# Rows for all partitions: products with a broadcast operand replaced by transfers inside the chip

## The chip, the cores and the metric

The kernel runs on one core of a Trainium2 chip. The metric is the device time of one execution in microseconds (us). All data are 32-bit floats.

## The reference

Two blocks run one after the other on x of [256 tokens, 1024]. What the change touches is this part of the first block (two layers) and of the second (one layer):

```python
# first block, per layer: forgetting attention (4 heads), beside differential and stick-breaking attention
logf = log_sigmoid(bf + b_forget[layer])
cum_logf = cumsum(logf, axis=1).transpose(0, 2, 1)          # [head, position]
logits = q @ k.T * scale + cum_logf[..., :, None] - cum_logf[..., None, :]
p = softmax(where(causal, logits, -inf))

# second block: state space heads (16 heads, chunks of 128), beside an attention with an index and a relative bias
acum = cumsum(dt * a, axis=1)
seg = acum[:, :, None] - acum[:, None, :]
lmat = exp(where(causal, seg, -inf))
wmat = cb[..., None] * lmat * dt[:, None]
y = einsum('bijgh,bjghp->bighp', wmat, x)                   # and the state carried from chunk to chunk

# attention of the second block: logits = q @ k.T * scale + rel_bias[bucket(t - s)], on the 64 best keys by an index
# then: x = x + g_f * moe(h), 32 experts of 1024 x 2048 and 1024 x 1024 each, four per token
```

Both parts need a row vector (a cumulative sum over the keys or the tokens of one head) beside a column vector on every one of the 128 partitions.

## The kernel before

Each engine has one program written out in order (`@block.tensor`, `@block.sync`, `@block.gpsimd`, `@block.scalar`, `@block.vector`); they meet at semaphores. Tokens are handled as two blocks of 128, features as chunks of 128 partitions. TensorE writes its results to seven PSUM banks used in turn: `take(name)` gives the next bank and waits until what it held seven takes ago is freed, `full(mm, name)` tells the others that it is ready, `ch.free(ins, name)` gives it back, `product(engine, name)` makes an engine wait for it.

Weights come in 2 MB groups through a ring of four slots. SP issues them in one written order (L1332 to L1336), each as soon as the group that held its slot was used (`slot_last`). The expert loads follow on the same queue; each waits for products of the mixer part or of earlier experts. Nine slots hold weights of experts.

*First block, per layer.* TensorE makes the projections, then the cumulative sums of the forget gate: `cumq` (the sum as a column, L771 to L773) and, for each of four heads, a [128, 256] bank with the sum as a row on all partitions: the operand `logf[:, b, h:h+1].broadcast_to([P, P])` against a triangular matrix (L779, L781, two heads to a bank, `cumk0` and `cumk1`). DVE makes `sf` from them (L1928), adds the mask, adds the stick-breaking sums `after0` to `after3` to `zs` (L1937) and the strict mask (the event `c_exponent`, for which ScalarE waits), and then adds the q k products `f0` to `f3` to `sf` (L1942). Maxima, exponents on ScalarE, division, and `turn_head(l, "f", h)` on TensorE (L548) follow. The value products of the differential heads are `head_value(l, "a", h)` (L554).

*Second block, state space stage.* `acumT` has the cumulative sums with heads on partitions (copied by DVE at L2025). A loop over p = 0 to 8 has, on TensorE, two products that copy the rows of heads 2p and 2p + 1 to all partitions (`A0` to `A15`, L969), then a projection of other work (`project_aside(p)`: q, kv, index keys, z), then the values of heads 2p - 2 and 2p - 1 (`ssm_values`). On DVE the same loop has `decay_in` for two heads (three operations on A each), then `decay_out` for the two heads before. ScalarE takes the exponents between the two, and copies what the asides made. Before this loop ScalarE copies `x_tok` out of four banks.

*The relative bias.* A [8, 512] table is written by POOL to DRAM 128 times (`bias_scratch`, source `biasrev` on eight partitions of `nine`), and SP loads it shifted into `bm` behind the weight group x2 (L1340 to L1348). DVE adds it near 581 us.

Of the kernel before, what the change touches and what calls it, by code (L numbers as in the profile page):

```python
# [86 lines left out]
def mixer_moe_kernel(nc, a, out):  # L87
# [23 lines left out]
    def sb(name, shape, dt=F32, where=ctx):  # L111
        return where.enter_context(nc.sbuf_tensor(name, shape, dt))
# [113 lines left out]
    mod_part = sb("mod_part", [P, 3, 512], where=first)  # L226
    pick_row = sb("pick_row", [P, 64], where=first)
    x_stats = sb("x_stats", [P, NB, 2, 6], where=first)
    x_mean = sb("x_mean", [P, NB, 2], where=first)
# [21 lines left out]
    bm = sb("bm", [P, 8, W3], where=second)  # L251
    cbs = early[:, NB * D:NB * D + 2 * W3].rearrange("p (g n) -> p g n", g=2)
    idx = sb("idx", [P, 4, W3], where=second)
    probT2 = idx[:, 0:2, :]
# [222 lines left out]
    def _(pe):  # L477
# [238 lines left out]
        for l in range(DEPTH):  # L716
# [57 lines left out]
            full(mm, f"{L}cumq")  # L774
            for h in range(HB):
                if h % 2 == 0:
                    bank = take(f"{L}cumk{h // 2}")
                c = h % 2 * T
                pe.matmul(bank[:, c:c + T], logf[:, 0, h:h + 1].broadcast_to([P, P]), up_ones[:, :],  # L779
                          start=True, stop=False)  # L780
                mm = pe.matmul(bank[:, c + P:c + T], logf[:, 1, h:h + 1].broadcast_to([P, P]), up,  # L781
                               start=False, stop=True)
                if h % 2:
                    full(mm, f"{L}cumk{h // 2}")
            pe.wait_ge(ev("log_fail"), l + 1)
# [175 lines left out]
        for p in range(SH // 2 + 1):  # L961
            if p < SH // 2:
                for h in (2 * p, 2 * p + 1):
                    if h == 0:
                        read_out(pe, "acumT")
                    bank = take(f"A{h}")
                    q = slice(32 * (h % 2), 32 * (h % 2) + 32)
                    at = 32 * (h % 2) + h
                    mm = pe.matmul(bank[:, 0:T], ident[q, at:at + 1].broadcast_to([32, P]), acumT[q, :],  # L969
                                   start=True, stop=True)  # L970
                    full(mm, f"A{h}")
                project_aside(p)
            if p == 1:
                read_out(pe, "xt11")
            if p >= 1:
                for h in (2 * p - 2, 2 * p - 1):
                    ssm_values(h)
# [349 lines left out]
    def _(sp):  # L1327
# [4 lines left out]
        for g, (name, src) in enumerate(groups):  # L1332
# [4 lines left out]
            if g == 1:  # L1337
                sp.dma_start(const_tiles[False][:, P:], packs[False][1][:, P:]).then_inc(ev("const_in"), 16)
                sp.dma_start(const_tiles[True][:, :], packs[True][1][:, :]).then_inc(ev("const_in"), 16)
            if name == "x2":  # L1340
                sp.wait_ge(ev("bias_out"), 16)
                sp.wait_ge(ev("h_ready"), 4 * DEPTH)
                for qb in range(NB):
# [108 lines left out]
    def _(act):  # L1452
# [82 lines left out]
        for l in range(DEPTH):  # L1535
# [36 lines left out]
            for b in range(NB):  # L1572
                read(f"{L}va{b}", va[:, b, :])
            read(f"{L}cv0", vbc[:, 0, 256:512], cols=slice(0, 256))
            act.wait_ge(ev("c_exponent"), l + 1)
# [49 lines left out]
        for i in range(2):  # L1625
            read(f"g{i}", ga[:, 2 * i:2 * i + 2, :])
        act.wait_ge(ev("xs"), 1)
        for b in range(NB):
# [141 lines left out]
    def _(dve):  # L1770
# [109 lines left out]
        for l in range(DEPTH):  # L1880
# [42 lines left out]
            ch.free(dve.tensor_copy(cumq[:, :], product(dve, f"{L}cumq")[:, 0:NB * HB]), f"{L}cumq")  # L1923
            for h in range(HB):
                name = f"{L}cumk{h // 2}"
                cum = product(dve, name)[:, h % 2 * T:(h % 2 + 1) * T]
                ts(sf[:, h, 0:P], cum[:, 0:P], -1.0, cumq[:, h:h + 1], ALU.mult, ALU.add)
                ins = dve.tensor_scalar(sf[:, h, P:W3], cum, -1.0, cumq[:, HB + h:HB + h + 1], ALU.mult, ALU.add)  # L1928
                if h % 2:
                    ch.free(ins, name)  # L1930
                else:
                    ch.after(ins)
            tt(sf[:, :, :], sf[:, :, :], over(K["row_mask"][:, :], HB), ALU.add)

            for h in range(HC):
                name = f"{L}after{h}"
                ch.free(dve.tensor_tensor(zs[:, h, :], product(dve, name)[:, 0:W3], zs[:, h, :], ALU.add), name)  # L1937
            tt(zs[:, :, :], zs[:, :, :], over(K["strict_add"][:, :], 4), ALU.add, ev("c_exponent"))

            for h in range(HB):  # L1940
# [103 lines left out]
        def decay_in(h):  # L2044

            A, d = product(dve, f"A{h}"), decay[:, h % 4, :]
            if h >= 4:
                dve.wait_ge(*values_done[("ssm", h - 4)])
            col = K["col_mask"][:, 0:P]
            stt(d[:, 0:P], A[:, 0:P], neg_acum[:, 0, h:h + 1], col, ALU.add, ALU.add)  # L2050
            ts(d[:, P:T], A[:, P:T], neg_acum[:, 2, h:h + 1], None, ALU.add)
            ch.free(dve.scalar_tensor_tensor(d[:, T:W3], A[:, P:T], neg_acum[:, 1, h:h + 1], col, ALU.add, ALU.add),
                    f"A{h}")
            ch.after(dve.tensor_copy(sink[:, :], d[:, 0:1]), ev("decay_exponent"))

# [264 lines left out]
```

## Time and profile before

| | |
|---|---|
| median of 3 runs | 1632.63 us (1631.58 to 1634.78) |
| the profiled execution | 1630.76 us, span 1628.8 us |
| mean granted TensorE clock | 0.995 of full speed |
| bytes read from DRAM | 511.21 MB, 316 GB/s over the span |
| first block | 0 to 376 us |
| second block up to the experts | 376 to 704 us |
| experts | 704 to 1623 us |

The span is the time from the first to the last instruction in the profile. PE is TensorE, PEld its weight loads, DVE VectorE, ACT ScalarE, POOL GpSimd; SPq, ACTq and POOLq are queues that issue transfers. A matmul of 32-bit data has several records ("x2" and "x4" count records). "Idle before" is the time that an engine stood still before an instruction, and the name behind the arrow is what it waited for.

### The profile page before, as it was taken

To read this page: it belongs to the slowest core of one execution; us is meant where nothing else is said; L and a number is where in the kernel's file an instruction comes from. 1 tells how busy PE (TensorE), PEld (TensorE's weight loads), DVE (VectorE), ACT (ScalarE), POOL (GpSimd) and SP (SyncE) were. 2 spreads that over 40 slices of the span, in tenths; PEclk is the share of its full clock that TensorE was granted. 3 is DMA by queue.
4 is the path that set the end of the run, shared out by engine and by line. 5 is a ranking of instruction groups with operands and counts; after the bars stand their busy time and mean duration, and the time that the engine had idled before them with its cause. 6 is when DMAs were issued, how large, how long until landed. Compare 5 with 4: busy or idle time off the path is not lost.

```text
span 1628.8 us, 18474 instructions
## 1 busy us (share of the span) xinstructions
PE 1544.0 (95%) x7521; PEld 873.4 (54%) x7521; DVE 451.1 (28%) x974; ACT 278.1 (17%) x552; POOL 21.4 (1%) x42
## 2 busy tenths in 40 slices
PE   7999999999999999999999999999999998999997
PEld 6768777786877878843333333333333333333232
DVE  2453643513346471131211111121112112111111
ACT  1244104324232531030000000000000000000000
POOL 4000000000000000000000000000000000000000
PEclk9999999999999999999999999999999999999999
DMA  9763994327333423689999999999999999999996
GB/s 260 194 203 104 339 333 153 107 103 256 128 118 104 144 93 136 280 336 421 428 429 425 428 428 426 430 426 429 427 429 427 426 429 426 430 425 428 426 427 292
DMA packets 84073, 515.19 MB, mean 316 GB/s; under 512 B 5444, under 2 KB 8804, under 8 KB 59440
## 3 DMA queue, kind: packets, MB, share of 16 engines
q1 hardware_dynamic: 81744, 511.35, 77.3%
q0 software_dynamic: 2240, 3.02, 1.9%
q8 instruction: 42, 0.69, 0.2%
q14 instruction: 15, 0.12, 0.0%
q10 hardware_dynamic: 32, 0.01, 0.0%
HBM read 511.21 MB, written 3.15 MB: 316 GB/s over the span
## 4 chain that ended last, share of the span: by engine, by line
PE 77%; DMA 15%; DVE 4%; ACT 2%; issue 1%; SPq 0%; ACTq 0%; another core or an unknown queue 0%; DVEq 0%
PE psum L514 25%; PE psum L1190 20%; PE psum L1287 11%; DMA ring<-in_w_gu 9%; DMA w_down<-in_w_gu 4%; PE psum L1168 4%; PE psum L523 4%; PE psum L1177 2%; PE psum L1135 2%; PE psum L554 1%; DMA ring<-in_w_ada 1%; DMA ring<-in_w_in 1%; PE psum L579 1%; DVE hidden L2266 1%; PE psum L1275 1%
## 5 line engine op out<-in xcount | busy, mean ns | idle before, releaser
L514 PE MATMUL psum<-spare,ring 128*128 128x256 f32 x1504 | 335.3, 382 | 2.8 <-ACT spare L1502 2.7
L514 PEld LDWEIGHTS psum<-spare,ring 128*128 128x128 f32 x1504 | 284.9, 191 | 51.6 <-issue 12.2
L1190 PE MATMUL psum<-ring,hg 128*64 128x512 f32 x1040 | 233.1, 596 | 6.5 <-DMA ring<-in_w_gu 6.5
L1190 PEld LDWEIGHTS psum<-ring,hg 128*64 128x64 f32 x1040 | 71.0, 137 | 155.2 <-issue 140.0
L1190 PE MATMUL psum<-w_down,hg 128*64 128x512 f32 x656 | 146.3, 596 | 4.7 <-DMA w_down<-in_w_gu 4.6
L2257 DVE TENSOR_SCALAR gu<-psum 128x512 f32<-128x512 f32 x32 | 22.1, 691 | 325.3 <-PE psum L1190 325.3
L2269 DVE TENSOR_TENSOR o_slot<-psum,gain_rows 128x512 f32<-128x512 f32 x32 | 22.1, 691 | 320.3 <-PE psum L1287 320.3
L1190 PEld LDWEIGHTS psum<-w_down,hg 128*64 128x64 f32 x656 | 44.9, 137 | 97.6 <-issue 88.6
L1287 PE MATMUL psum<-ring,hiddenT 128*64 128x512 f32 x352 | 78.0, 595 | 9.5 <-ACT hiddenT L1737 7.2
L1287 PE MATMUL psum<-w_down,hiddenT 128*64 128x512 f32 x352 | 78.0, 595 | 9.5 <-ACT hiddenT L1737 7.2
L1731 ACT ACTIVATE putT<-psum 128x256 f32<-128x256 f32 x32 | 12.3, 383 | 381.7 <-PE psum L1197 381.6
L1733 ACT ACTIVATE hidden<-gu 128x512 f32<-128x512 f32 x32 | 20.2, 630 | 297.9 <-DVE gu L2257 297.9
L1168 PEld LDWEIGHTS psum<-pick,h_tok 128*128 128x128 f32 x512 | 60.0, 196 | 11.7 <-issue 11.4
L1177 PE MATMUL psum<-o_slot,putT 64*128 64x512 f32 x256 | 63.6, 615 | 0.8 <-DVE o_slot L2269 0.8
L1168 PE MATMUL psum<-pick,h_tok 128*128 128x128 f32 x512 | 63.0, 283 | 0.2 <-DVE passes L2221 0.2
L523 PE MATMUL psum<-ring,spare 128*128 128x260 f32 (+2 forms) x192 | 56.9, 453 | 0.5 <-DMA ring<-in_w_in 0.5
L514 PE MATMUL psum<-yT,ring 128*128 128x256 f32 x256 | 55.6, 379 | 0.0
L1287 PEld LDWEIGHTS psum<-ring,hiddenT 128*64 128x64 f32 x352 | 26.2, 137 | 54.2 <-issue 54.2
L1287 PEld LDWEIGHTS psum<-w_down,hiddenT 128*64 128x64 f32 x352 | 26.2, 137 | 54.2 <-issue 54.2
L514 PEld LDWEIGHTS psum<-yT,ring 128*128 128x128 f32 x256 | 48.6, 190 | 6.6
L523 PEld LDWEIGHTS psum<-ring,spare 128*128 128x128 f32 x192 | 35.9, 190 | 18.7 <-issue 14.3
L1177 PEld LDWEIGHTS psum<-o_slot,putT 64*128 64x128 f32 x256 | 22.0, 186 | 41.9 <-issue 40.2
(421 smaller groups left out, 1457.7 us busy)
## 6 DMA issues: line engine op xcount, KB each, us to landing
ring<-in_w_gu SPq DMA_DIRECT2D x65, 2048.0 KB, 28.3
w_down<-in_w_gu SPq DMA_DIRECT2D x41, 2048.0 KB, 28.4
ring<-in_w_in SPq DMA_DIRECT2D x24, 2048.0 KB, 9.5
w_down<-in_w_dn SPq DMA_DIRECT2D x22, 2048.0 KB, 28.7
ring<-in_w_dn SPq DMA_DIRECT2D x22, 2048.0 KB, 31.6
ring<-in_w_ada SPq DMA_DIRECT2D x12, 2048.0 KB, 8.9
spare<-in_w_gu SPq DMA_DIRECT2D x11, 2048.0 KB, 28.2
nine<-in_w_gu SPq DMA_DIRECT2D x11, 2048.0 KB, 29.7
```

The costliest lines, as they stand in the source:

```text
L514: mm = pe.matmul(bank[0:m, c * T:(c + 1) * T], w[:, k, c0 + c * P:c0 + c * P + m], src[:, k, :], start=(i == 0), stop=(i == k_n - 1))
L523: mm = pe.matmul(bank[:, 0:n], src[:, k, blk * P:(blk + 1) * P], w[:, k, c0:c0 + n], start=(k == 0), stop=(k == k_n - 1))
L554: pe.matmul(bank[rows, c * T:(c + 1) * T], v[:, 0, cols], wT[:, 0:T], start=True, stop=False)
L579: mm = pe.matmul(bank[:, 0:T], ones_d, wide[:, c, :], start=(c == 0), stop=(c == KC - 1))
L1135: pe.matmul(psum[:, loop_bank(4 + part), :], bias_row[r, side, :, :].rearrange("p h s -> p (h s)"), b_gu[r, :], start=True, stop=False, sk ...
L1168: mm = pe.matmul(psum[:, loop_bank(first_bank + part), j * P:j * P + width * CAP], h_tok[:, b, c * P:(c + 1) * P], pick[:, b, 0:width, :], ...
L1177: mm = pe.matmul(psum[:, loop_bank(2 * b + half), :], putT[r, side, b * P:(b + 1) * P], o_slot[r, :], start=False, stop=False, skip_group_ ...
L1190: mm = pe.matmul(psum[half * CAP:(half + 1) * CAP, loop_bank(4 + part), :], hg[:, k, side, :], w[:, c0:c0 + 512], start=False, stop=(k == ...
L1287: mm = pe.matmul(psum[half * CAP:(half + 1) * CAP, loop_bank(7), :], hiddenT[:, c, j * CAP:(j + 1) * CAP], tile[:, c0:c0 + 512], start=(k ...
L1733: act.activation(hidden[:, 0, :], gu[:, 0, :], ACT.Sigmoid, scale=1.702).then_inc(ev("g_sig"), 1)
L2257: dve.tensor_scalar(gu[:, 0, :], psum[:, loop_bank(4), :], 7.0, None, ALU.min).then_inc(ev("g_in"), 1)
L2269: dve.tensor_tensor(o_slot[:, :], psum[:, loop_bank(7), :], gain_rows[:, :], ALU.mult).then_inc(ev("o_slot"), 1)
```

## The change

In a layer of the first block one bank `cumk` takes the place of two: two products make the sums of all four heads as four rows. ScalarE copies the rows to SBUF (`forget_rows`, partitions 0 to 3 of `lam_in`), then issues four transfers, each of which reads one row 128 times and writes it to all partitions (`forget_all`, in the buffer `qk`). DVE handles `zs` first, then waits for the four transfers and makes `sf` from `forget_all`. In the second block the sixteen `A` products go; ScalarE issues sixteen such transfers from rows 0 to 15 of `acumT`, twelve into `bm` and four into `k2`, ahead of its copies of `x_tok`. DVE waits for four heads at a time. The small copy to `sink` in `decay_in` goes, and the load of the relative bias moves from behind group x2 to behind group kvup, after the twelfth `decay_exponent`, since `bm` is in use until then.

```diff
--- before.py
+++ after.py
@@ -225,6 +225,8 @@
     cumq = sb("cumq", [P, NB * HB], where=first)
     mod_part = sb("mod_part", [P, 3, 512], where=first)
     pick_row = sb("pick_row", [P, 64], where=first)
+    forget_rows = lam_in[:, :, :].rearrange("p a b -> p (a b)")[0:HB, 0:T]
+    forget_all = qk[:, 0:HB, :]
     x_stats = sb("x_stats", [P, NB, 2, 6], where=first)
     x_mean = sb("x_mean", [P, NB, 2], where=first)
     x_rstd = sb("x_rstd", [P, NB], where=first)
@@ -250,6 +252,8 @@
     x_tok = early[:, 0:NB * D].rearrange("p (b d) -> p b d", b=NB)
     bm = sb("bm", [P, 8, W3], where=second)
     cbs = early[:, NB * D:NB * D + 2 * W3].rearrange("p (g n) -> p g n", g=2)
+    A_late = k2[:, :, :]
+    A_first = bm[:, :, :].rearrange("p h n -> p (h n)").rearrange("p (h t) -> p h t", t=T)
     idx = sb("idx", [P, 4, W3], where=second)
     probT2 = idx[:, 0:2, :]
     decay = idx
@@ -772,16 +776,10 @@
             pe.matmul(bank[:, HB:2 * HB], ones, logf[:, 0, :], start=True, stop=False)
             mm = pe.matmul(bank[:, HB:2 * HB], up, logf[:, 1, :], start=False, stop=True)
             full(mm, f"{L}cumq")
-            for h in range(HB):
-                if h % 2 == 0:
-                    bank = take(f"{L}cumk{h // 2}")
-                c = h % 2 * T
-                pe.matmul(bank[:, c:c + T], logf[:, 0, h:h + 1].broadcast_to([P, P]), up_ones[:, :],
-                          start=True, stop=False)
-                mm = pe.matmul(bank[:, c + P:c + T], logf[:, 1, h:h + 1].broadcast_to([P, P]), up,
-                               start=False, stop=True)
-                if h % 2:
-                    full(mm, f"{L}cumk{h // 2}")
+            bank = take(f"{L}cumk")
+            pe.matmul(bank[0:HB, 0:T], logf[:, 0, :], up_ones[:, :], start=True, stop=False)
+            mm = pe.matmul(bank[0:HB, P:T], logf[:, 1, :], up, start=False, stop=True)
+            full(mm, f"{L}cumk")
             pe.wait_ge(ev("log_fail"), l + 1)
             for h in range(HC):
                 bank = take(f"{L}after{h}")
@@ -960,15 +958,6 @@
 
         for p in range(SH // 2 + 1):
             if p < SH // 2:
-                for h in (2 * p, 2 * p + 1):
-                    if h == 0:
-                        read_out(pe, "acumT")
-                    bank = take(f"A{h}")
-                    q = slice(32 * (h % 2), 32 * (h % 2) + 32)
-                    at = 32 * (h % 2) + h
-                    mm = pe.matmul(bank[:, 0:T], ident[q, at:at + 1].broadcast_to([32, P]), acumT[q, :],
-                                   start=True, stop=True)
-                    full(mm, f"A{h}")
                 project_aside(p)
             if p == 1:
                 read_out(pe, "xt11")
@@ -1337,9 +1326,9 @@
             if g == 1:
                 sp.dma_start(const_tiles[False][:, P:], packs[False][1][:, P:]).then_inc(ev("const_in"), 16)
                 sp.dma_start(const_tiles[True][:, :], packs[True][1][:, :]).then_inc(ev("const_in"), 16)
-            if name == "x2":
+            if name == "kvup":
                 sp.wait_ge(ev("bias_out"), 16)
-                sp.wait_ge(ev("h_ready"), 4 * DEPTH)
+                sp.wait_ge(ev("decay_exponent"), 12)
                 for qb in range(NB):
                     width = (qb + 1) * P
                     src = bass.AP(tensor=bias_dram[:, :, :].tensor, offset=T - 1 - qb * P,
@@ -1571,6 +1560,10 @@
             f(small[:, 8:16], small[:, 8:16], ACT.Ln, ev("forget_ln"), bias=1.0)
             for b in range(NB):
                 read(f"{L}va{b}", va[:, b, :])
+            read(f"{L}cumk", forget_rows, cols=slice(0, T), rows=slice(0, HB))
+            for h in range(HB):
+                act.dma_start(forget_all[:, h, :], forget_rows[h:h + 1, :].rearrange("o (x t) -> o x t", x=1).broadcast_to([1, P, T]))\
+                    .then_inc(ev("forget_rows"), 16)
             read(f"{L}cv0", vbc[:, 0, 256:512], cols=slice(0, 256))
             act.wait_ge(ev("c_exponent"), l + 1)
             f(zs[:, :, :], zs[:, :, :], ACT.Exp, ev("wc"))
@@ -1624,6 +1617,10 @@
         f(dtx[:, 3, :], dtx[:, 2, :], ACT.Ln, ev("dt_ln"))
         for i in range(2):
             read(f"g{i}", ga[:, 2 * i:2 * i + 2, :])
+        read_out(act, "acumT")
+        for h in range(SH):
+            A = A_first[:, h, :] if h < 12 else A_late[:, h - 12, :]
+            act.dma_start(A, acumT[h:h + 1, :].rearrange("o (x t) -> o x t", x=1).broadcast_to([1, P, T])).then_inc(ev(f"decay_rows{h // 4}"), 16)
         act.wait_ge(ev("xs"), 1)
         for b in range(NB):
             for j in range(2):
@@ -1921,21 +1918,17 @@
             weigh_a(3)
 
             ch.free(dve.tensor_copy(cumq[:, :], product(dve, f"{L}cumq")[:, 0:NB * HB]), f"{L}cumq")
-            for h in range(HB):
-                name = f"{L}cumk{h // 2}"
-                cum = product(dve, name)[:, h % 2 * T:(h % 2 + 1) * T]
-                ts(sf[:, h, 0:P], cum[:, 0:P], -1.0, cumq[:, h:h + 1], ALU.mult, ALU.add)
-                ins = dve.tensor_scalar(sf[:, h, P:W3], cum, -1.0, cumq[:, HB + h:HB + h + 1], ALU.mult, ALU.add)
-                if h % 2:
-                    ch.free(ins, name)
-                else:
-                    ch.after(ins)
-            tt(sf[:, :, :], sf[:, :, :], over(K["row_mask"][:, :], HB), ALU.add)
-
             for h in range(HC):
                 name = f"{L}after{h}"
                 ch.free(dve.tensor_tensor(zs[:, h, :], product(dve, name)[:, 0:W3], zs[:, h, :], ALU.add), name)
             tt(zs[:, :, :], zs[:, :, :], over(K["strict_add"][:, :], 4), ALU.add, ev("c_exponent"))
+
+            dve.wait_ge(ev("forget_rows"), 16 * HB * (l + 1))
+            for h in range(HB):
+                for cols, q in PARTS:
+                    ts(sf[:, h, cols], forget_all[:, h, 0:P + P * q], -1.0, cumq[:, HB * q + h:HB * q + h + 1],
+                       ALU.mult, ALU.add)
+            tt(sf[:, :, :], sf[:, :, :], over(K["row_mask"][:, :], HB), ALU.add)
 
             for h in range(HB):
                 name = f"{L}f{h}"
@@ -2043,15 +2036,14 @@
 
         def decay_in(h):
 
-            A, d = product(dve, f"A{h}"), decay[:, h % 4, :]
+            dve.wait_ge(ev(f"decay_rows{h // 4}"), 64)
+            A, d = A_first[:, h, :] if h < 12 else A_late[:, h - 12, :], decay[:, h % 4, :]
             if h >= 4:
                 dve.wait_ge(*values_done[("ssm", h - 4)])
             col = K["col_mask"][:, 0:P]
             stt(d[:, 0:P], A[:, 0:P], neg_acum[:, 0, h:h + 1], col, ALU.add, ALU.add)
             ts(d[:, P:T], A[:, P:T], neg_acum[:, 2, h:h + 1], None, ALU.add)
-            ch.free(dve.scalar_tensor_tensor(d[:, T:W3], A[:, P:T], neg_acum[:, 1, h:h + 1], col, ALU.add, ALU.add),
-                    f"A{h}")
-            ch.after(dve.tensor_copy(sink[:, :], d[:, 0:1]), ev("decay_exponent"))
+            stt(d[:, T:W3], A[:, P:T], neg_acum[:, 1, h:h + 1], col, ALU.add, ALU.add, ev("decay_exponent"))
 
         def decay_out(h):
             d, cb = decay[:, h % 4, :], cbs[:, h // 8, :]
```

## Rows read from the trace of the kernel before

**Rows 1.** Page, part 1: engine, busy us (share of the span), instructions.

```profile
PE 1544.0 (95%) x7521; PEld 873.4 (54%) x7521; DVE 451.1 (28%) x974; ACT 278.1 (17%) x552; POOL 21.4 (1%) x42
```

**Rows 2.** Chain of waits, in order of time: start us, length us, what.

```profile
108.64 0.54 PE psum L779 x2
...
111.37 0.65 PE psum L788 x2
...
124.17 0.43 PE psum L554 x2
...
134.35 0.65 PE psum L548 x6
...
581.41 3.37 DVE bm L1774
...
587.65 5.50 PE psum L532 x16
...
1275.96 34.91 DMA ring<-in_w_gu
```

**Rows 3.** Timeline of DVE, layer 0: start us, length us, line and operation.

```profile
113.79 1.76 DVE L1774 TENSOR_TENSOR sf<-sf,k_all 128x1536 f32<-128x1536 f32 x1
...
119.74 2.33 DVE L1942 SCALAR_TENSOR_TENSOR sf<-psum,sf 128x384 f32<-128x384 f32 x4
...
128.31 2.81 DVE L1778 TENSOR_SCALAR sf<-sf,row_sum 128x128 f32<-128x128 f32 x8
```

**Rows 4.** Timeline of ACT, layer 0.

```profile
128.26 1.01 ACT L1460 ACTIVATE probT<-psum 128x384 f32<-128x384 f32 x2
```

**Rows 5.** Timelines of PE and of DVE, state space stage.

```profile
452.86 0.70 PE L969 MATMUL psum<-acumT,k_all 32*128 32x256 f32 x4
453.49 7.17 PE L514 MATMUL psum<-spare,ring 128*128 128x256 f32 x32
...
468.32 0.66 PE L554 MATMUL psum<-idx,sc 128*64 128x256 f32 x4
...
525.32 7.17 PE L514 MATMUL psum<-spare,ring 128*128 128x256 f32 x32
...
451.26 0.42 DVE L2025 COPY acumT<-psum 128x256 f32<-128x256 f32 x1
...
508.45 1.78 DVE L1782 SCALAR_TENSOR_TENSOR idx<-idx,dt,sc 128x256 f32<-128x256 f32 x4
```

**Rows 6.** Groups by line, 452 to 526 us: busy us, mean ns, idle us before, releaser.

```profile
L969 PE MATMUL psum<-acumT,k_all 32*128 32x256 f32 x32 | 6.3, 426 | 0.6 <-DVE xbc L2066 0.6
...
L941 PE MATMUL psum<-spare,ring 128*64 128x256 f32 x32 | 3.7, 381 | 0.7 <-DVE xbc L2066 0.7
...
L2052 DVE SCALAR_TENSOR_TENSOR idx<-psum,neg_acum,k_all 128x128 f32<-128x128 f32 x16 | 5.6, 351 | 0.6
```

**Rows 7.** Transfers of 40:100, 440:560, the whole span: KB each, us to landing.

```profile
ring<-in_w_in SPq DMA_DIRECT2D x3, 2048.0 KB, 38.9
bias_scratch<-nine POOLq DMA_DIRECT2D x1, 2048.0 KB, 47.5
...
ring<-in_w_in SPq DMA_DIRECT2D x5, 2048.0 KB, 8.9
...
out<-h_tok SPq DMA_DIRECT2D x4, 256.0 KB, 2.9
...
k_all<-c_all SPq DMA_DIRECT2D x1, 64.0 KB, 1.9
```

**Rows 8.** Timeline of ACT, its queue's first issue: start us, length us.

```profile
0.72 0.60 ACTq L1468 DMA_DIRECT2D vec_rows<-in_ln_in_g  x1
```

**Rows 9.** Stretches: length, busy us by engine (count), PEclk, DMA share, GB/s.

```profile
74.00:82.00 8.00, 8.00 (x46) 6.78 (x46) 2.21 (x2) 3.64 (x10) 0.00 (x0) 1.00 0.50 69
92.00:100.00 8.00, 7.53 (x22) 3.85 (x21) 1.14 (x2) 5.67 (x7) 0.00 (x0) 1.00 1.03 376
...
585.00:592.00 7.00, 6.58 (x20) 5.14 (x21) 6.69 (x10) 0.00 (x0) 0.00 (x0) 0.55 0.46 188
```

## The prediction

> **What bounds the kernel now.** I read the page first: TensorE is busy for 95% of the span [rows 1]. Then the chain of waits, in order of time: up to about 700 us it is nearly all TensorE products in program order, and from 1276 us on it is made of waits for expert weights of about 35 us each [rows 2]. In the expert part the loads run without a pause, and the first of them are released by products of the mixer, so what the mixer part (0 to 700 us) gains or loses moves those loads and the end with it, one for one. All that the change touches lies in the mixer part. So I looked in the timelines at two places per edit: when TensorE needs the result, and how much slack stands before that. Last I read the table of transfers, for one whose source lies in few partitions. There is one, the write of the bias table, and it decides the forecast.
>
> **The products removed.** In a layer, eight products (L779, L781) fill the chain from 108.64 to 111.37, 2.73 us; the two that stay are one head's pair, 0.68 us [rows 2]. So TensorE has 2.05 us less per layer, 4.1 us in both. In the state space stage sixteen products of acumT go. A pair of them puts off the next product by 0.63 us (452.86 to 453.49) [rows 5], together 5.0 us. Two waits of TensorE for a bank that DVE frees, 0.6 and 0.7 us [rows 6], go too, since sixteen fewer banks are taken. If nothing else moved: 4.1 + 5.0 + 1.3 = 10.4 us faster.
>
> **What a copied row costs.** Each new transfer reads one row of 1 KB from one partition, 128 times, 128 KB in all; four per layer from partitions 0 to 3, sixteen later from partitions 0 to 15, in that order. No such copy stands in the trace. The nearest rows:
> - bias_scratch<-nine reads eight rows of eight partitions again and again, 2048 KB, and takes 47.5 us, 44 GB/s; a weight load of the same 2048 KB over 128 partitions takes 8.9 us [rows 7]. Between 74 and 82 us the DMA engines are only half in use and move 69 GB/s, loads included; without the write it is 376 GB/s [rows 9]. Loads in flight beside the write took 38.9 us [rows 7].
> - out<-h_tok, 256 KB from all partitions, lands in 2.9 us, and 64 KB of constants in 1.9 us [rows 7]. I take 1.9 us as the fixed part; the difference, 1.0 us, is eight rows of 2 KB one after another on each of sixteen engines, so one partition gives at least 16 GB/s.
>
> So a row of 128 KB costs between 3.0 us (all of the write's 44 GB/s is there for one row) and 8.2 us (16 GB/s). Below 3.0 us it is only if the write was held up at its DRAM side; that is a rival. The write had two neighbouring groups of four partitions at work at once, the queued copies have one group at a time. If the limit belongs to such a group, a copy gets half of 44 GB/s and takes 6.0 us, and somewhat less because the write's engines also served loads. I take c = 5.0 us (26 GB/s).
>
> The Trainium skill (SBUF — State Buffer, section Door 1: The DMA port swizzle) says that partitions 0 to 3 and 32 to 35 share one of 16 ports, of about 27 GB/s each, which speaks against this change. An estimate by that page is 4.8 us per row; the write's 44 GB/s from eight partitions, two such ports, agrees. By 4.8 us the sum below would be 50 us instead of 54.
>
> **A layer, with c.** The product ends at 109.3, ScalarE's copy of it takes 0.5, issue and fixed part 1.9: the four rows are there at L = 111.7 + 4c. DVE stands at the new wait from about 115 (the adds to zs and the strict mask now come first) and then has eight tensor_scalars (2.8), the mask (1.8) and the first of four adds of f (0.6) [rows 3]: L + 5.2. Behind the wait are queued those adds, and TensorE's first value product (L554, 124.17 before) takes the bank that the first of them frees. From it to the first turned forget row (L548, 134.35) TensorE has 10.2 us [rows 2], so that comes at L + 15.5. ScalarE just keeps up: its reads of two turned rows end at 129.3 [rows 4], 9.5 us after the adds of f begin [rows 3], so at L + 14.1. The delay of a layer is 111.7 + 4c + 15.5 - 134.35 = 4c - 7.15; with c = 5.0 12.85 us, for both layers 25.7 us.
>
> **The state space stage.** acumT is there at 451.7 [rows 5], the last group of four rows at 451.7 + 1.9 + 16c. Then come DVE's exponents of two heads (six operations of 0.35 and their gaps, 2.3) [rows 6], the weightings of the pair before, which stand behind the wait in DVE's order (1.8), and on TensorE one pair of values (0.8), the z product and a small one (7.5) and two pairs of values (1.6) [rows 5]: 14.0. The stage ended at 525.3 [rows 5], so the delay is 453.6 + 16c + 14.0 - 525.3 = 16c - 57.7; with c = 5.0 22.3 us. The earlier groups (at 473.6, 493.6, 513.6) hold TensorE up as well, but the last one ends last. The removed products and waits lie inside these stalls and save nothing then.
>
> **The clock.** After 3.5 us of idle time the granted clock was 0.55 in 585 to 592 us [rows 9], mostly its level of 1.2 GHz. Sixteen products in that stretch took 5.50 us [rows 2], 0.34 each; at the full clock thirty-two take 7.17 [rows 5], 0.22 each. So such a stall costs 2.0 us more, and three stalls set the end (two layers, last group): 6 us.
>
> **Edits at nothing.** An issue takes ScalarE up to 0.60 us [rows 8], sixteen of them up to 9.6; behind them wait its four copies of x, of which TensorE needs the first bank at about 460.6 (one q product of 7.1 us behind 453.5). At 9.6 us that copy would end near 462 and cost 1.3 us, at 0.4 us each nothing; I take nothing, the stalls cover it. In a layer the four issues lie before a copy that ScalarE makes several us later, and it idles till then. The sixteen small copies to sink go, off the path. The bias load moves to where twelve exponents are done; its consumer stands at 581.4 [rows 2], more than 50 us later, and both move. On SP's queue the g1 load waits behind it; its products come after the stage's end and after the z products. Were its cover gone, the bias load would cost what a load of its size takes, at most 8.9 us. If weight loads run four times slower beside the copies, as beside the write, those in flight (z0, z1) take some 40 us and still arrive before their products. POOL's queue is not passed.
>
> **Sum.** 25.7 + 22.3 + 6 = 54 us slower. The profiled execution took 1630.76 us (span 1628.8), 1.9 below the median of the three runs, 1632.63; on the median the forecast is 1686.6 us. In general the change is 24c - 66: 42 at 4.5 us per row, 83 at 6.2. At c = 3.0 the stage is bound by TensorE again and gains 6.3, the layers lose 9.7 and 4 of clock: 7 us slower, 1640. At 8.2 it is 131 us, 1764.
>
> **Rivals.**
> - *The copies run at full rate*, c up to 1.3 us (each would land as the 256 KB do): all is hidden and the removed products count, 10.4 us faster, 1622.2. For it: the slow write ended in DRAM, and no copy inside the chip is in the trace. Against it: outputs written to DRAM land in 2.9 us without such a limit [rows 7], and the write held just half of the engines. The new waits decide: below c = 1.8 us in the layers and 3.6 in the stage they cost nothing. Chance 0.12.
> - *The loss and the gain meet*, c about 1.7 to 2.6 us (50 to 77 GB/s for one row): within 3.3 us of 1632.6. Chance 0.05.
> - *Sixteen engines at one partition get even less than eight at eight*, or weights arrive late behind the copies: 1725 to 1764. For it: the loads beside the write at over four times their time. Against it: the loads in flight have that much slack. Chance 0.03.
> - *Forecast*, the limit of few source partitions, 1640 to 1725: 0.80.
>
> The Trainium skill (DMA: Bandwidth & Descriptors, section Where 436 GB/s comes from) says that transfers from SBUF to SBUF are bound by the fabric at 435 GB/s; by that page alone the first rival, 1622.2, would be the forecast, and no run here shows such a transfer yet.
>
> **The numbers.** The range is that of the forecast's case, which holds 0.80. What a measurement of this kernel can tell from no change is about 0.2%, 3.3 us. Slower 0.83, same 0.05, faster 0.12.
>
> **What would show it.** In the profile after: the landing times of the copies to forget_all (qk) and to A's rows (bm, k2); four rows about 20 us after the first issue, sixteen about 80. DVE's wait for them before the eight tensor_scalars, TensorE idle for 10 to 15 us at L554's place in each layer and before the values of heads 0, 2, 6 and 10; DMA share high with under 100 GB/s. If the rows land within 4 us of their issue, the limit of the write was at its DRAM side and the forecast is wrong with its sign.

## The result and the profile after

The changed kernel takes 1708.26 us (median of 4 executions, 1705.68 to 1710.64); the kernel before, run on the same chip, 1633.41 us (1631.58 to 1634.78). The ratio is 1.046, its 95% interval 1.0448 to 1.0474: 74.9 us slower. The forecast was 1686.6 us, 54 us slower. The profiled execution after took 1710.64 us, with a span of 1708.8 us.

The page of the kernel after; the second line is the queue of ScalarE's transfers (packets, MB, share of 16 engines), the third is a group of projections with its idle time, most of it behind ScalarE:

```profile
PE 1542.9 (90%) x7465; PEld 871.5 (51%) x7465; DVE 446.3 (26%) x958; ACT 279.0 (16%) x554; POOL 21.2 (1%) x42
...
q10 hardware_dynamic: 3488, 3.16, 4.4%
...
L518 PE MATMUL psum<-spare,ring 128*128 128x256 f32 x1504 | 340.1, 386 | 53.4 <-ACT sc L1449 49.8
```

TensorE's busy time is the same as before to 1.1 us [rows 1]; its share fell from 95% to 90%, so the loss is idle time (84.8 us before, 165.9 after). Lines have new numbers after: value products L558 and L559 (L554, L555 before), turned rows L552 (L548), projections L518 (L514).

The chain of waits after, layer 0, against [rows 2] (start us, length us, what):

```profile
120.25 3.46 PE psum L527 x16
123.70 14.32 issue
138.02 1.19 PE psum L558 x2
...
150.85 0.65 PE psum L552 x6
```

and the timelines of ScalarE's queue, DVE and TensorE, layer 0 and the state space stage:

```profile
111.20 3.15 ACTq L1565 DMA_DIRECT2D qk<-lam_in  x4
...
132.73 1.38 DVE L1774 TENSOR_SCALAR sf<-qk,cumq 128x128 f32<-128x128 f32 x4 [15.90 <-DMA qk<-lam_in]
...
484.64 0.42 DVE L2018 COPY acumT<-psum 128x256 f32<-128x256 f32 x1
485.15 38.70 ACTq L1623 DMA_DIRECT2D bm<-acumT  x12
...
505.98 0.35 DVE L1779 SCALAR_TENSOR_TENSOR idx<-bm,neg_acum,k_all 128x128 f32<-128x128 f32 x1 [19.02 <-DMA bm<-acumT]
...
523.87 18.27 ACTq L1623 DMA_DIRECT2D k<-acumT  x4
542.25 2.48 ACT L1449 ACTIVATE sc<-psum 128x512 f32<-128x512 f32 x4 [60.63 <-issue]
542.99 10.18 PE L518 MATMUL psum<-spare,ring 128*128 128x256 f32 x32 [49.78 <-ACT sc L1449]
```

In the layer all is as forecast: the issues are short (3.15 us for four), DVE stands 15.9 us at the new wait, and 14.3 us of TensorE's time go behind it. Four rows were there 21.5 us after the first issue; less the fixed 1.9 that is c = 4.9 us per row (c is the time of one copied row). In the stage the first four rows were there after 20.8 us, c = 4.7; all sixteen were there after 68.3 us (the last issue began at 537.4 and landed 16.1 us later), which is 4.15 us per row on average. But look at the last two lines: ScalarE's first copy of x starts at 542.25, 57 us after the first issue. It waited for no data; its own sixteen issues lasted that long. The chain shows them one by one:

```profile
485.15 0.48 ACTq L1623
485.66 0.62 ACTq L1623
486.31 1.76 ACTq L1623
488.10 5.28 ACTq L1623
493.41 4.78 ACTq L1623
498.22 4.79 ACTq L1623
```

Two are as short as an issue of the kernel before [rows 8]; from the fourth on nearly each lasts as long as a row takes. TensorE needed the copies of x after one projection and stood 49.78 us. The stage's transfer rate, slice by slice of 2 us, from 480 to 560 us:

```profile
GB/s 5 250 410 381 64 28 27 26 29 27 26 39 62 28 27 28 27 27 41 40 63 27 28 27 27 28 27 52 34 28 27 28 28 27 26 27 13 204 409 394
```

The rows move at 27 GB/s, with short stretches of about 62 near 505 and 521 us and of 52 near 535, where by the landings one group of four partitions ends and the next begins. That is why sixteen rows took less than sixteen times 4.7 us.

To compare all kernels I take three intervals from each timeline: in each layer from the first product of `logf` to the first turned forget row, and in the stage from DVE's copy of acumT to the last value product. Behind the stage nothing differs: from there to the end of the profiled execution it is 1105.8 us before and 1105.8 after.

| kernel | median, us | layer 0 | layer 1 | stage |
|---|---|---|---|---|
| before | 1633.41 | 26.27 | 26.27 | 73.69 |
| after | 1708.26 | 41.45 | 41.95 | 120.16 |
| e1_layers | 1661.00 | 40.76 | 41.57 | 73.68 |
| e2_stage | 1679.35 | 26.27 | 26.27 | 118.90 |
| e3_pool | 1673.67 | 41.55 | 41.16 | 85.01 |
| e4_spread | 1643.78 | 26.22 | 30.40 | 79.80 |
| e5_near | 1718.49 | 41.34 | 41.82 | 130.64 |
| e6_far | 1691.78 | 41.96 | 41.28 | 103.26 |
| e7_spread_pool | 1625.28 | 26.27 | 26.27 | 67.12 |
| e8_own_row | 1633.36 | 28.17 | 28.24 | 72.77 |
| e9_order | 1639.77 | 28.91 | 30.53 | 73.67 |
| e11_woven | 1677.95 | 41.04 | 41.74 | 89.57 |

The layers after are 15.2 and 15.7 us late, the stage 46.5: 77.3 us in all, where the medians say 74.9. The three intervals account for the difference of medians within 3.1 us in every kernel of the table. Their runs of the kernel before had medians of 1630.6 to 1631.6 us.

### The profile page after: what moved, and what is told of

Same layout as the page of the kernel before. It is cut to its first block, busy times and chain, and to the rows that moved or that the text cites. A ratio compares the mean times of both kernels' runs of the same rounds, so it can differ in the third digit from the quotient of the medians.

```text
span 1708.8 us, 18366 instructions
## 1 busy us (share of the span) xinstructions
PE 1542.9 (90%) x7465; PEld 871.5 (51%) x7465; DVE 446.3 (26%) x958; ACT 279.0 (16%) x554; POOL 21.2 (1%) x42
## 3 DMA queue, kind: packets, MB, share of 16 engines
HBM read 511.21 MB, written 3.15 MB: 301 GB/s over the span
## 4 chain that ended last, share of the span: by engine, by line
PE 71%; DMA 16%; DVE 4%; ACTq 3%; issue 3%; ACT 2%; SPq 0%; another core or an unknown queue 0%; DVEq 0%
PE psum L518 23%; PE psum L1179 19%; PE psum L1276 11%; DMA ring<-in_w_gu 8%; DMA w_down<-in_w_gu 4%; PE psum L1157 4%; PE psum L527 3%; ACTq L1623 3%; DMA ring<-in_w_in 2%; PE psum L1166 2%; PE psum L1124 2%; PE psum L558 1%; DMA ring<-in_w_ada 1%; PE psum L583 1%; DVE hidden L2258 1%
## 5 line engine op out<-in xcount | busy, mean ns | idle before, releaser
L518 PE MATMUL psum<-spare,ring 128*128 128x256 f32 x1504 | 340.1, 386 | 53.4 <-ACT sc L1449 49.8
L518 PEld LDWEIGHTS psum<-spare,ring 128*128 128x128 f32 x1504 | 288.5, 194 | 103.0 <-issue 61.2
L518 PE MATMUL psum<-yT,ring 128*128 128x256 f32 x256 | 55.6, 379 | 0.0
L518 PEld LDWEIGHTS psum<-yT,ring 128*128 128x128 f32 x256 | 48.6, 190 | 6.6
L527 PEld LDWEIGHTS psum<-ring,spare 128*128 128x128 f32 x192 | 35.9, 190 | 19.3 <-issue 14.3
```

The lines of the kernel that those rows point to most:

```text
L518: mm = pe.matmul(bank[0:m, c * T:(c + 1) * T], w[:, k, c0 + c * P:c0 + c * P + m], src[:, k, :], start=(i == 0), stop=(i == k_n - 1))
L527: mm = pe.matmul(bank[:, 0:n], src[:, k, blk * P:(blk + 1) * P], w[:, k, c0:c0 + n], start=(k == 0), stop=(k == k_n - 1))
```

## The experiments

**One part alone.** e1_layers keeps the layers' transfers and has the stage's products and the bias load as before; e2_stage is the reverse.

```diff
 e1_layers, against after
+                for h in (2 * p, 2 * p + 1):   # the A products are back
-        for h in range(SH):
-            act.dma_start(A, acumT[h:h + 1, :]...)
 ...
 e2_stage, against after
+            for h in range(HB):                # the cumk products are back
-            for h in range(HB):
-                act.dma_start(forget_all[:, h, :], forget_rows[h:h + 1, :]...)
 ...
```

> The layer part alone: forget rows by transfers in both layers, the stage's sixteen products and the bias load as in the kernel before. In the trace of the changed kernel the four rows of a layer are there 21.5 us after their first issue and the turned forget rows come 15.2 us late. Theory A (the copies are slow because one row is read from one partition, c = 4.9 us each, and nothing else of the change matters in a layer): the same 15 us per layer, about 1633.4 + 30 = 1663 us, and the transfers about 510 ns for each packet of 1 KB as in the full change. Rival (the layers' copies are slow only beside something that the stage part brings, or their delay is absorbed by slack later in the mixer): under 1645 us.

> The stage part alone, with the bias load moved: A's rows by sixteen transfers, the layers as in the kernel before. Theory A (the stage is 46.5 us late by itself, of which about 21 by the rows' own time and the rest because ScalarE's queue is held 57 us by its issues): 1633.4 + 46 = 1679 us, and the loss of this kernel and of the layer part alone add up to the 74.9 us of the full change within 4 us. Rival (part of the stage's delay comes from what the layers' delay shifts onto it, loads that collide): the two losses add up to clearly less than 74.9, this one below 1665 us.

e1_layers: 1661.0 us, ratio 1.0173 (1.0154 to 1.0191), 29.9 us slower. e2_stage: 1679.35 us, ratio 1.0279 (1.0256 to 1.0303), 48.2 us slower. The sum is 78.1, against 74.9. The parts are separate and add up; the layers were forecast right, the stage not.

**The hold of ScalarE's queue.** e3_pool lets GpSimd issue the stage's sixteen copies:

```diff
+        read_out(pool, "acumT")
+            pool.dma_start(A, acumT[h:h + 1, :]...)
-        read_out(act, "acumT")
-            act.dma_start(A, acumT[h:h + 1, :]...)
```

> The full change, but the stage's sixteen copies are issued by GpSimd instead of ScalarE; sources, targets, sizes and waits are the same. Theory A (in the full change ScalarE cannot issue more than three or four outstanding copies and stands 57 us, so that TensorE waits 49.8 us for its copies of x; the rows themselves would cost 16c - 57.7, 20 us at c = 4.9, and 2 us of clock): 20 to 25 us faster than the full change, about 1685 us, and TensorE's long wait for ScalarE is gone, with waits for the rows of heads 4, 8 and 12 in its place. Rival 1 (the hold costs nothing of its own, the rows set the end either way): 1705 to 1710 us. Rival 2 (GpSimd, held in the same way, delays its own work that TensorE or DVE needs): as slow or slower than the full change, with a wait for GpSimd in the trace.

It took 1673.67 us, ratio 1.0253 (1.0234 to 1.0272), 34.6 us below the changed kernel; 20 to 25 were expected. Timelines of GpSimd's queue, DVE and TensorE:

```profile
481.45 6.38 POOL L1436 DMA_DIRECT2D bm<-acumT  x12 [435.86 <-DVE acumT L2018]
...
487.82 2.12 POOL L1436 DMA_DIRECT2D k<-acumT  x4
...
502.68 0.35 DVE L1779 SCALAR_TENSOR_TENSOR idx<-bm,neg_acum,k_all 128x128 f32<-128x128 f32 x1 [19.62 <-DMA bm<-acumT]
...
508.04 1.55 PE L558 MATMUL psum<-idx,sc 128*64 128x256 f32 x3 [11.83 <-issue]
```

GpSimd issues sixteen in 8.5 us and isn't held. But this queue also ran the rows otherwise. It used a third of the packets (768 for 2.10 MB, against 2304 on ScalarE's queue). The first four rows were there after 21.2 us, as late as in the changed kernel, but all sixteen after 54 us instead of 68, or 3.3 us a row on average. So it changed two things, and I made one that changes the hold alone. In e11_woven ScalarE copies x first and then spreads its issues among the exponents:

```diff
-        for h in range(SH): (sixteen issues, then the copies of x)
+        (the copies of x first)
+        for h in range(7):
+            decay_row(h)
...
         for h in range(SH):
             f(decay[:, h % 4, :], ..., ACT.Exp, ev("decay_exp"))
+            if h + 7 < SH:
+                decay_row(h + 7)
```

> The full change with the stage's sixteen transfers still issued by ScalarE, from one partition each, but in another order: ScalarE first makes its four copies of x, then issues seven rows, and one more row behind each of the first nine exponents. The rows are as slow as in the full change. Theory A (the hold of ScalarE's queue is what the prediction missed, the rows' own time is what it had in its sum): the stage is 16c - 57.7 = 19 to 21 us late at c = 4.8 to 4.9, and 2 us of clock, instead of 46.5: about 1685 us. It tells the hold apart from the rows' rate, which in the version issued by GpSimd changed as well. Rival (the weaving only moves the waits, each exponent waits behind an issue that waits for a row): 1700 us or more.

1677.95 us, ratio 1.0288 (1.0271 to 1.0305): 47.3 us above the kernel before instead of 74.9. Timeline:

```profile
480.93 2.49 ACT L1449 ACTIVATE sc<-psum 128x512 f32<-128x512 f32 x4 [2.18 <-PE psum L901]
...
483.45 21.08 ACTq L1627 DMA_DIRECT2D bm<-acumT  x7
...
509.70 1.55 PE L558 MATMUL psum<-idx,sc 128*64 128x256 f32 x3 [12.45 <-issue]
...
525.26 0.69 PE L558 MATMUL psum<-idx,sc 128*64 128x256 f32 x2 [4.36 <-DVE idx L1785]
```

The issues are held as before (seven in 21 us), the rows are as slow (the second group is used 17.8 us after the first, 4.5 us per row), but the copies of x no longer stand behind the issues. Some exponents still do, for up to 7.9 us. The stage is 15.9 us late instead of 46.5. So the rows' own time costs at most 15.9 us, and the other 30.6 us are the price of the place where ScalarE issues them. DVE waited for rows twice, for the first group (20.24 us) and the second (11.63 us), and for no later one.

**What makes a row slow.** e4_spread keeps number, size and targets of all transfers and lets each read from many partitions that hold the same row. For this DVE first copies the log forget gates 32 times, two more operations per layer:

```diff
+            act.dma_start(forget_all[:, h, :], forget_rows[h:P:HB, :]...)   # 32 partitions
+            act.dma_start(A, acumT[h:P:SH, :]...)                           # 8 partitions
```

> The full change with the same number of transfers, targets, bytes and issues by ScalarE, but each transfer reads its row from many partitions that all hold it: 32 partitions in the layers (one product gives 128 rows, each head 32 times, from a copy of log forget by VectorE), 8 partitions in the stage (acumT holds each head 8 times). Theory A (a row is slow because one partition, or its port, gives only about 27 GB/s): a layer's four rows are there within 4 us of the first issue, the stage's sixteen in under 20 us (c about 1.2 us or less), ScalarE is held far less, and the kernel comes near the kernel before or below it: 1622 to 1640 us. Rival (transfers inside SBUF of 1 KB pieces are slow wherever they read, on the write side or in the engines): c stays 4.8 us and the time 1700 to 1710 us.

1643.78 us, ratio 1.0063 (1.0044 to 1.0083): above the 1640 of theory A, far from the rival's 1700. A layer's four rows were there 8.7 us after their first issue (112.40), not within 4 as expected; in layer 1 TensorE stood 2.84 us behind them. Timelines, layer 0 and stage:

```profile
121.08 2.81 DVE L1778 TENSOR_SCALAR sf<-qk,cumq 128x128 f32<-128x128 f32 x8 [3.26 <-DMA qk<-lam_in]
...
459.74 12.52 ACTq L1626 DMA_DIRECT2D bm<-acumT  x12
...
472.30 4.36 ACTq L1626 DMA_DIRECT2D k<-acumT  x4
476.76 2.48 ACT L1452 ACTIVATE sc<-psum 128x512 f32<-128x512 f32 x4 [20.55 <-issue]
```

With eight source partitions the sixteen issues take 16.9 us, 1.05 us per row, and the hold falls from 57 to 17 us. So the source decides. Whether it is the partition or a group of them, two more kernels tell, each with two source partitions:

```diff
+            act.dma_start(A, acumT[h:h + 33:32, :]...)   # e5_near: h and h + 32
+            act.dma_start(A, acumT[h:h + 65:64, :]...)   # e6_far: h and h + 64
```

> The full change, but each of the stage's sixteen transfers reads its row from two partitions that hold it, h and h + 32, 64 times each; transfers, bytes, targets and issues are the same. Theory A (the limit belongs to a group of partitions; the Trainium skill, SBUF — State Buffer, section Door 1: The DMA port swizzle, puts h and h + 32 on one port): nothing changes, c stays 4.8 us, packets of 1 KB about 465 ns, 1705 to 1711 us. Rival (the limit belongs to the single partition): c halves to 2.4 us, ScalarE is held about 30 us instead of 57, and the time is about 1681 us.

> As the kernel with h and h + 32, but the two partitions are h and h + 64. Both theories of the limit (a group of partitions with h and h + 64 in different groups; a single partition) expect c of 2.4 us, ScalarE held about 30 us. With the full change (57 us of hold, stage 46.5 us late) and the version with eight source partitions (17 us, 6.1 us late) a microsecond of hold costs about one, so the stage is about 19 us late and the time about 1681 us. Rival (the slow rows come of the write side, or of the repeated read of one address): 1705 us or more. Together with the kernel before: only one different from the other means a group, both near 1681 a partition, both near 1708 neither.

e5_near 1718.49 us, ratio 1.0526 (1.0508 to 1.0544); e6_far 1691.78 us, ratio 1.0369 (1.0351 to 1.0386). The stretch from 490 to 515 us of the one and then of the other (last three numbers: PEclk, DMA share, GB/s):

```profile
490.00:515.00 25.00, 0.66 (x4) 0.23 (x2) 3.96 (x12) 0.00 (x0) 0.00 (x0) 0.61 0.11 27
```

```profile
490.00:515.00 25.00, 0.00 (x0) 0.00 (x0) 3.96 (x12) 0.00 (x0) 0.00 (x0) 0.57 0.14 46
```

In both, about two of the sixteen DMA engines are at work (shares 0.11 and 0.14). Near gives 27 GB/s, the same as one partition; far gives 46. The limit belongs to a group that holds h and h + 32, not h + 64. This agrees with the map of the Trainium skill (SBUF — State Buffer, section Door 1: The DMA port swizzle), whose figure of about 27 GB/s per port the runs show too. Two expectations were missed: near came out 10 us slower than the full change, because ScalarE was held 67.6 us instead of 57, from the third issue on; and far did not halve the row's time but took it to 2.8 us, 46 GB/s. Whether the two engines or the two groups set these 46 GB/s is not shown.

**All at full rate.** e8_own_row copies every partition's own row, so all 128 are read once. Like e4_spread it has the extra copies of the log forget gates. Left out: the rows are not the heads' rows, and acumT is the constant -1000.

```diff
+                act.dma_start(forget_all[:, h, :], forget_rows[:, :])
+            act.dma_start(A, acumT[:, :])
```

> The full change as in the version with spread sources, but every transfer copies each partition's own row to the same partition, in layers and stage, so all 128 partitions are read once each. Left out: the rows are not the heads' rows, and acumT holds the constant -1000 (the decays become zero); instructions, bytes and issues are the same. It tests the first rival of the prediction, copies at full rate. Theory A: a row takes about 0.6 us, an issue; ScalarE is held 10 us in the stage and costs 1 to 3 us there; 10.4 us of products and waits are saved: 1622 to 1628 us. Rival (TensorE's removed work was not on the path, or fixed times of transfer, issue and the shared engines eat it): 1630 us or more, with DVE waiting for the rows in a layer although they are read at full rate.

1633.36 us, ratio 1.0007 (0.9995 to 1.0018): the rival's case. Timeline:

```profile
109.09 2.52 ACTq L1568 DMA_DIRECT2D qk<-lam_in  x4
...
118.04 2.81 DVE L1777 TENSOR_SCALAR sf<-qk,cumq 128x128 f32<-128x128 f32 x8 [3.54 <-DMA qk<-lam_in]
...
122.68 2.33 DVE L1940 SCALAR_TENSOR_TENSOR sf<-psum,sf 128x384 f32<-128x384 f32 x4
...
123.34 0.69 PE L559 MATMUL psum<-probT,va 128*128 128x256 f32 x2 [1.96 <-issue]
```

and, of this run and then of the kernel before, the stretch from the first value product on (PEclk third from the end):

```profile
123.30:127.00 3.70, 3.66 (x15) 3.46 (x16) 3.55 (x5) 0.00 (x0) 0.00 (x0) 0.58 0.00 0
```

```profile
124.00:128.00 4.00, 4.00 (x25) 3.66 (x24) 0.23 (x2) 3.65 (x17) 0.00 (x0) 1.00 0.00 0
```

The rows come 8.9 us after the first issue even so, beside a weight load in flight, and DVE waits 3.54 us; each layer is 1.9 us slower than before, not 2.05 faster. TensorE gives back what it saved: it stands 1.96 us before the first value product, which begins 16.25 us after the first product of `logf`, against 16.09 before. The rest of the loss lies behind this stall, where the granted clock is 0.58 instead of 1.00. The stage gains only 0.9, since sixteen issues still hold ScalarE 11 us and TensorE stands 3.73 us for the copies of x; its next projection then takes 8.83 us instead of 7.17.

**The moves alone.** e9_order is the kernel before with its products, and only the order of DVE's work in a layer and the place of the bias load changed.

```diff
+            for h in range(HC):   # adds to zs and strict mask come first
             for h in range(HB):   # then sf from the products
-            if name == "x2":
+            if name == "kvup":
+                sp.wait_ge(ev("decay_exponent"), 12)
```

> The kernel before with the two moves of the change alone: in the layers VectorE's adds to zs and the strict mask come ahead of its operations on the forget rows (which stay products), and the bias load waits for twelve exponents ahead of kvup. Theory A (the prediction's edits at nothing: VectorE has slack in this stretch, the bias load's consumer stands later): within 3 us of the kernel before. Rival (holding two product banks longer, or the later load on SP's queue, costs): 3 us or more slower, TensorE waiting for a bank at the values of a layer, or for bm<-bias_scratch or the g1 load.

1639.77 us, ratio 1.005 (1.0037 to 1.0064), 8.6 us slower; theory A fell. The stage is as before (73.67), and the changed kernel, which moves the bias load too, takes the same 1105.8 us behind it as the kernel before, so the bias load costs nothing that shows. The layers are 2.6 and 4.3 us late. Timelines of DVE and TensorE in layer 0:

```profile
109.05 0.17 DVE L1923 COPY cumq<-psum 128x8 f32<-128x8 f32 x1 [3.39 <-PE psum L773]
112.64 0.56 DVE L1926 TENSOR_TENSOR zs<-psum,zs 128x384 f32<-128x384 f32 x1 [3.43 <-PE psum L789]
...
119.47 0.48 PE L540 MATMUL psum<-bc_qk 64*128 64x128 f32 x2 [0.87 <-DVE sf L1933]
...
121.28 0.50 PE L540 MATMUL psum<-bc_qk 64*128 64x128 f32 x4 [0.89 <-DVE sf L1933]
```

DVE now stands 3.43 us, because it takes the products first that are made last. So it reads the two banks of forget sums later and frees them later. TensorE needs these banks for its q k products and stands twice, 0.87 and 0.89 us, in both layers; in layer 1 the granted clock also falls to 0.88 (302 to 314 us). This is the rival's case. The value products do not wait: DVE's adds of f start at 123.05 instead of 119.74 [rows 3], still before TensorE gets to the values at 126.95.

**A version below both.** e7_spread_pool keeps the layers' products and makes the stage's rows by transfers from eight partitions, issued by GpSimd.

```diff
+            pool.dma_start(A, acumT[h:P:SH, :]...)
```

> The stage's rows alone by transfers, each from eight partitions, issued by GpSimd; the layers have their products as before. Theory A (what cost time were the single source partition and the hold of ScalarE; both gone, the sixteen products and two waits for banks, 5.0 and 1.3 us, are saved): 1626 to 1631 us, below the kernel before. Rival (the first four rows come later than the first products did, and TensorE waits for the first pair of values): no gain or a loss of some us, 1632 to 1640, with a wait of DVE for bm<-acumT of 5 us or more and TensorE idle behind it before the first values.

> The version with the stage's rows from eight partitions, issued by GpSimd, and the layers' products as before, once more with more executions. It was 6.3 us faster than the kernel before, as much as sixteen products and two waits for banks (5.0 + 1.3 us): again 1624 to 1628 us, 0.2 to 0.5% below the kernel before. Rival (that difference was of start-up times, which vary by some us from run to run): within 0.2%.

1625.28 us, ratio 0.9951 (0.9935 to 0.9968), and in e10_again, the same kernel, 1625.63 us, ratio 0.9963 (0.995 to 0.9977). Timeline and stretch:

```profile
453.22 7.06 POOL L1442 DMA_DIRECT2D bm<-acumT  x12 [407.29 <-DVE acumT L2025]
...
460.73 0.35 DVE L1782 SCALAR_TENSOR_TENSOR idx<-bm,neg_acum,k_all 128x128 f32<-128x128 f32 x1 [5.90 <-DMA bm<-acumT]
```

```profile
454.00:468.00 14.00, 14.00 (x68) 12.07 (x68) 6.56 (x18) 2.84 (x6) 8.61 (x15) 1.00 0.86 197
```

DVE waits 5.9 us for the first rows, as the rival had it, but TensorE is busy all 14 us with two projections. The stage is 6.6 us shorter; sixteen products and two waits were priced at 6.3.

## Why the prediction was right, and where it was not

- **What bounds the kernel: right.** What the mixer part loses moves the end one for one (1105.8 us behind the stage, before and after).
- **What a copied row costs: right.** c was taken as 5.0 us; the layers give 4.9, the stage 4.7. What failed to hold is that all sixteen rows go at this pace: they took 4.15 us each on average. The choice rested on the write of the bias table being slow at its source and not in DRAM; e4_spread, e5_near and e6_far show that a copy inside the chip is limited at its source. Of the two pages that the prediction cites, the port map agrees with the runs. The Trainium skill (DMA: Bandwidth & Descriptors, section Where 436 GB/s comes from) has transfers from SBUF to SBUF bound by the fabric at 435 GB/s; one or two source partitions gave 27 and 46 GB/s here, and the measurement decides.
- **A layer: right.** 12.85 us and 2 of clock forecast, 15.2 and 15.7 measured. TensorE's value products behind the stall took 1.19 us instead of 0.43 in the chain, and in 134 to 150 us the granted clock was 0.72.
- **The stage: mis-sized by 22 us.** Forecast 22.3 and 2 of clock, measured 46.5. The step that failed is the one of the edits at nothing: it priced the sixteen issues at up to 0.60 us each, 9.6 in all, and took nothing for them. They lasted 57 us, and this hold costs 30.6 us (after against e11_woven). The term that was in the sum, the rows' own time, was 8 us too large (24.3 for at most 15.9 in e11_woven): with 4.15 us per row instead of 5.0, 16c - 57.7 is 8.7 us, and the last group no longer ended last. In e11_woven the stalls are those of the first group (12.45 us of TensorE) and the second (4.36). The two errors have opposite signs; that the total of 54 for 74.9 is nearer than the stage alone, 24.3 for 46.5, is partly luck.
- **Products removed: half right.** In the stage they are worth what was said once nothing else is in the way (6.6 us in e7_spread_pool for 6.3). In a layer no run gained by them. In e8_own_row, with rows at full rate, 8.95 us less the fixed 1.9 are c = 1.76 us, just the threshold of 1.8 below which the prediction saw no cost. The value products were as late as before, so the threshold was about right for the wait; but the stall of 1.96 us brought the lower clock, and that made the layer 1.9 us slower. The first rival took c up to 1.3 us and 10.4 us of gain; the run made for its case took 1633.36 us, not 1622.2.
- **The new order of DVE's work** was priced at nothing, and that holds in the changed kernel: DVE was through with `zs` at 116.8 us, 15.9 us before the rows came, and ScalarE, not DVE, frees the bank of the forget sums; TensorE's chain has no wait between 109.39 and 123.70. With the products in place the same order costs 6.9 us in both layers (e9_order), because they hold two banks longer. That cost does not carry over to the changed kernel.
- **The bias load moved:** nothing, as forecast.

What stays open: which part of a transfer counts against a queue's room. ScalarE stood after about three rows from one partition and after two in e5_near. And why GpSimd's queue had sixteen rows done after 54 us instead of 68 was not looked into. All sixteen were outstanding there after 8.5 us, so more groups of source partitions could be read at once; that is an argument, and no run tests it.

## What to carry to other kernels

A transfer has a source side: when it reads few partitions, count the groups that these lie in and not its bytes, and spread the source over copies of the row where they exist anyway. An engine that issues transfers can be held by them as long as they run, so its urgent work goes first, or another engine issues. An instruction removed from TensorE is worth its time only if what TensorE waits for next comes no later than before: compare when the replacement is there with when TensorE would now need it.

## What the hardware showed unexpectedly

- ScalarE's queue took few transfers ahead: sixteen issues lasted 57 us with rows of 4.8 us, 67.6 with rows of about 4.9 from two partitions, 40.6 with rows of 2.8, 16.9 with rows of 1.05, and 10.9 (mostly 0.62 each) when all partitions were read. GpSimd issued sixteen in 8.5 us with rows of one partition and in 9.4 with those of eight partitions.
- At a step from one group of four source partitions to the next, the rate rose from 27 to about 62 GB/s for some 2 us, as if two groups served at once.
- Sixteen engines at one source partition (share 0.78 in 490 to 500 us of the changed kernel) got no more than two in e5_near (share 0.11): 27 GB/s in both. Two engines at two groups got 46.
- Behind a stall of TensorE of 1.96 us the granted clock was 0.58 over 3.7 us (e8_own_row); before the stall it was 1.00.
